# An expert loop's gated units ahead of a weight tile's halves, in two queues

## The chip, the cores and the metric

One core of a Trainium2 chip runs the kernel. Its engines, each with an instruction queue of its own, are TensorE (PE), VectorE (DVE), ScalarE (ACT), GpSimd (POOL) and SyncE (SP, which here only issues transfers). The metric is the device time of one execution in microseconds (us). A difference is told as the median of the runs of one kernel against that of the other.

## What is computed

The reference is a network in float32 on 256 tokens of width 1024: two blocks of convolution, state-space scan and a mixture of experts, and then four blocks of other mixers with dense feed-forward layers. The change lies in the mixture of experts, once in each of the first two blocks ("layer 0" and "layer 1" below):

```python
def expert(acc, ew):
    wg, wu, wd, cw = ew
    hid = jax.nn.silu(t @ wg) * (t @ wu)
    return acc + (cw[:, None] * (hid @ wd)).astype(acc.dtype), None
# 16 experts of width 256; each token is routed to two experts of one group of four
```

## The kernel before

**Split products.** A float32 matrix product is made of three products of a shorter float format. Each operand is cut into a high half (a rounded copy) and a low half (the operand less its high half): `mm3` (L752) issues high x high, high x low and low x high (L754, L755, L756). So each weight tile that arrives from memory is first split. ScalarE writes the high half (`make_high`, L1420, its copy is L1428), and then the low half is a subtraction (`make_low`, L416, its operation is L424). In the expert stages that subtraction is cut in two: VectorE takes the first 1024 columns, GpSimd the other 1024, both released by ScalarE's semaphore `high`. The tiles of the down projection are split in the same way by `make_down_high` (L1434) and `make_down_low` (L433), 512 columns on each of the two engines.

**Tokens by expert.** Tokens are scattered into 16 blocks of 128 rows, one block per expert. An expert's 256 hidden units are two slices of 128, so a layer has 32 slices: the even slice `j` and the odd slice `j + 1` of one expert are called a pair here. A slice has one gate-up weight tile (1 MB, 128 partitions x 2048) and one down tile (512 KB, 128 x 1024). The loop `slices_loop` (L435) runs `one(j, g)` on every engine; four slices are one turn of a hardware loop. Each engine runs its own list in its own order, and only semaphores tie them.

**TensorE's list** (`one`, L1096): at an even slice the rows of the next expert are transposed (`turn_rows`, L1062). Then the first half of the gate-up product of slice `j + 1` (12 matmuls), the transposition of the hidden rows of slice `j` (`turn_hidden`, L1079), the second half of the gate-up product of `j + 1`, and the down product of slice `j` (6 matmuls of 512 columns). The gate-up product of a slice waits for both low halves of its tile, VectorE's and GpSimd's (`low_ready`, L408).

**ScalarE's list** (`one`, L1653): the activation of the gate (L1655, releases `gate_act`), the high half of the tile of slice `j + 2` (L1428), the high half of the transposed hidden rows (L1659, waits for `hid_turned`, which TensorE's L1079 releases), at an even slice the high half of the next expert's rows (L1637), the high half of the next down tile (L1434), and at an odd slice `store`: it waits for the pair's down product, copies it out of PSUM (L1646) and issues a transfer (L1651).

**VectorE's list** (`one`, L2393): gate times up (L2395, releases `hid_raw`), the low half of the tile of slice `j + 2` (L424), the low half of the hidden rows (L2399, waits for `hid_high`, which L1659 releases; it releases `hidden`, for which the down product waits), the low half of the next expert's rows (L2390), the low half of the next down tile (L433).

**GpSimd's list** (`one`, L612): the transfer of an expert's rows (L610), its part of the low half of the tile of slice `j + 2` (L424), its part of the low half of the down tile of `j + 1` (L433).

Two buffers hold high halves (`HIGH`), four hold loaded tiles (`RING`). In the profile some names are those of the memory underneath: `border` is the activation `gact` and the raw hidden rows, `border_halves` the split hidden rows `hid`, `HT_halves` the split expert rows, `ssdb` the output rows, `zs_b` the arriving rows, `bank` a PSUM bank. The second expert stage of a layer, for overflowing experts, is skipped in this run: L1655 runs 64 times, 32 per layer.

Of the kernel before, what the change touches and what calls it, by code (L numbers as in the profile page):

```python
# [32 lines left out]
P = 128  # L33
# [29 lines left out]
RING = 4  # L63
QUAD = 32
HIGH = 2
TCOLS = 2 * P
# [134 lines left out]
def program(nc, dram, out, known):  # L201
# [4 lines left out]
    def sem(name):  # L206
        if name not in sems:
            sems[name] = ctx.enter_context(nc.semaphore(name))
            count[name] = 0
        return sems[name]  # L210
# [12 lines left out]
    def loop_base(name, key, total):  # L223

        sem(name)
        seen[name, key] = count[name]
        count[name] += total
        return seen[name, key]

    def base(name, key):  # L230
        sem(name)
        return known.get((name, key), 0)

    with ctx:
# [43 lines left out]
        ps = [ctx.enter_context(nc.psum_tensor(f"bank{b}", [P, 512], F32)) for b in range(8)]  # L278
# [15 lines left out]
        def view(buf, off, *shape):  # L294
            x = buf[:, off:off + int(np.prod(shape))]
            names = "abcd"[:len(shape)]
            if len(shape) == 1:
                return x
            return x.rearrange(f"p ({' '.join(names)}) -> p {' '.join(names)}",
                               **dict(zip(names[:-1], shape[:-1])))  # L300
# [30 lines left out]
        hid = view(border_r, 0, 2, 2, T)  # L331
# [8 lines left out]
        r = lambda x: x.bitcast(F32R)  # L340
# [75 lines left out]
        def make_low(eng, engine, c, g=0):  # L416

            at_ = slice(0, CUT[c]) if engine == "dve" else slice(CUT[c], TILE)
            if at_.start == at_.stop:
                return  # L420
            w, h = ring[SPLIT[c] % RING][:, at_], high[c % HIGH][:, at_]
            eng.wait_ge(sem("high"), c + 1 + RING * g)
            low = r(ring_r[SPLIT[c] % RING][:, at_])
            eng.tensor_tensor(low, w, h, ALU.subtract).then_inc(sem(f"low_{engine}"), 1)  # L424
# [985 lines left out]
        def _(act):  # L1410
# [9 lines left out]
            def make_high(c, g=0):  # L1420

                if c >= len(SPLIT):
                    return
                t = SPLIT[c]
                act.wait_ge(sem(f"tile_loaded{t % RING}"), 16 * (t // RING + 1) + 16 * g)
                if c >= HIGH:
                    act.wait_ge(sem("tile_free"), SPLIT[c - HIGH] + 1 + RING * g)
                nc.scalar.copy(r(high[c % HIGH][:]), ring[t % RING][:]).then_inc(sem("high"), 1)  # L1428

            def make_down_high(d, g=0):  # L1430
                act.wait_ge(sem(f"down_loaded{d % RING}"), 16 * (d // RING + 1) + 16 * g)
                if d >= HIGH or not isinstance(g, int):
                    act.wait_ge(sem("down_free"), d - HIGH + 1 + RING * g)
                nc.scalar.copy(r(dhigh[d % HIGH][:]), dring[d % RING][:]).then_inc(sem("down_high"), 1)  # L1434
# [190 lines left out]
            def experts(name, blocks, row0):  # L1625
                t0, c0, d0, slices = TILE_AT[name], SPLIT_AT[name], DOWN_AT[name], PER_BLOCK * blocks
                turned0, hid_turned0 = base("x_turned", name), base("hid_turned", name)
                taken0 = loop_base("out_taken", name, blocks)
                stored0 = [loop_base(f"y_stored{p}", name, 16 * blocks // 2) for p in range(2)]
                loop_base("gate_act", name, slices)  # L1630
                loop_base("x_high", name, blocks)
                loop_base("hid_high", name, slices)

                def split_rows(b, g):
                    act.wait_ge(sem("x_turned"), turned0 + b + 1 + RING // 2 * g)
                    for n in range(2):
                        i = nc.scalar.copy(r(xT[:, b % 2, 0, 4 * n:4 * n + 4, :].rearrange("p a b -> p (a b)")), ps[6 + n][:])  # L1637
                    i.then_inc(sem("x_high"), 1)

                def store(b, g):  # L1640

                    act.wait_ge(sem("down_free"), d0 + 2 * b + 2 + RING * g)
                    if stored0[b % 2] or b >= 2 or not isinstance(g, int):
                        act.wait_ge(sem(f"y_stored{b % 2}"), stored0[b % 2] + 16 * (b // 2) + 16 * g)
                    for n in range(2):
                        i = nc.scalar.copy(yrows[:, b % 2, n * D // 2:(n + 1) * D // 2], ps[2 * (b % 2) + n][:])  # L1646
                    i.then_inc(sem("out_taken"), 1)
                    act.wait_ge(sem("out_taken"), taken0 + b + 1 + RING // 2 * g)
                    dst = y_slots[row0 + P * b:row0 + P * b + P] if isinstance(g, int) else \
                        y_slots[bass.ds(row0 + P * b + 2 * P * g, P)]  # L1650
                    act.dma_start(dst, yrows[:, b % 2, :]).then_inc(sem(f"y_stored{b % 2}"), 16)  # L1651

                def one(j, g):  # L1653
                    act.wait_ge(sem("tile_free"), t0 + j + 1 + RING * g)
                    act_fn(gact[:, j % 2, 0:P], ps[4 + j % 2][:, 0:P], ACT.Silu).then_inc(sem("gate_act"), 1)  # L1655
                    if j + 2 < slices:
                        make_high(c0 + j + 2, g)
                    act.wait_ge(sem("hid_turned"), hid_turned0 + j + 1 + RING * g)
                    nc.scalar.copy(r(hid[:, j % 2, 0, 0:P]), ps[4 + j % 2][:, TCOLS:TCOLS + P]).then_inc(sem("hid_high"), 1)  # L1659
                    if j % 2 == 0 and j // 2 + 1 < blocks:  # L1660
                        split_rows(j // 2 + 1, g)
                    if j + 1 < slices:
                        make_down_high(d0 + j + 1, g)
                    if j % 2:
                        store(j // 2, g)

                if name[0] == "over":
                    for a in range(2):
                        make_high(c0 + a)
                make_down_high(d0)  # L1670
                split_rows(0, 0)
                slices_loop(act, slices, one, 0 if taken0 else 1)

            def moe(l, blocks):
# [246 lines left out]
        def _(dve):  # L1921
# [458 lines left out]
            def experts(name, blocks):  # L2380
                c0, d0, slices = SPLIT_AT[name], DOWN_AT[name], PER_BLOCK * blocks
                act0, high0, hid_high0 = (base(x, name) for x in ("gate_act", "x_high", "hid_high"))
                for n, total in (("x_split", blocks), ("hid_raw", slices), ("hidden", slices)):
                    loop_base(n, name, total)

                def split_rows(b, g):
                    dve.wait_ge(sem("x_high"), high0 + b + 1 + RING // 2 * g)
                    for n in range(2):
                        hi, lo = (xT[:, b % 2, i, 4 * n:4 * n + 4, :].rearrange("p a b -> p (a b)") for i in range(2))
                        i = tt(r(lo), ps[6 + n][:], hi, ALU.subtract)  # L2390
                    i.then_inc(sem("x_split"), 1)

                def one(j, g):  # L2393
                    dve.wait_ge(sem("gate_act"), act0 + j + 1 + RING * g)
                    tt(hrows[:, j % 2, :], gact[:, j % 2, 0:P], ps[4 + j % 2][:, P:TCOLS], ALU.mult).then_inc(sem("hid_raw"), 1)  # L2395
                    if j + 2 < slices:
                        make_low(dve, "dve", c0 + j + 2, g)
                    dve.wait_ge(sem("hid_high"), hid_high0 + j + 1 + RING * g)
                    tt(r(hid[:, j % 2, 1, 0:P]), ps[4 + j % 2][:, TCOLS:TCOLS + P], hid[:, j % 2, 0, 0:P], ALU.subtract)\  # L2399
                        .then_inc(sem("hidden"), 1)  # L2400
                    if j % 2 == 0 and j // 2 + 1 < blocks:
                        split_rows(j // 2 + 1, g)
                    if j + 1 < slices:
                        make_down_low(dve, "dve", d0 + j + 1, g)

                if name[0] == "over":
                    for a in range(2):
                        make_low(dve, "dve", c0 + a)
                make_down_low(dve, "dve", d0)
                split_rows(0, 0)  # L2410
                slices_loop(dve, slices, one)

            def moe(l, blocks):
# [533 lines left out]
```

## Time and profile before

| | |
|---|---|
| median of 3 runs | 2509.26 us (2508.42 to 2522.15) |
| the profiled execution | 2514.59 us, its span 2512.9 us |
| TensorE, VectorE, ScalarE, GpSimd busy | 2159.1, 1591.7, 1115.9, 475.6 us |
| loop of layer 0: GpSimd's first and last L424 start | 460.08 and 635.52 us |
| loop of layer 1: the same | 968.29 and 1153.02 us |

Busy time is the sum over instructions of one engine. A row of the trace's timeline has the start, the duration, the engine, the line, what it writes and reads, and in brackets how long the engine had been idle before it and what released it. Start times count from the start of the span.

### The profile page before, as it was taken

The numbers are of one execution on the slowest core, as the hardware profiler recorded it, in microseconds if no ns is written. First come the engines' busy times: TensorE is split into PE (matmuls) and PEld (weight loads), VectorE is DVE, ScalarE is ACT, GpSimd is POOL, SyncE is SP. The second block draws the span as 40 slices with busy tenths as digits, with TensorE's granted clock in tenths as the row PEclk, the third lists the DMA queues.
The fourth block names the chain that finished last, engine by engine and source line by source line (L and its number), as shares of the span: only waits on it lengthen the run. The fifth ranks groups of instructions, "written<-read, shape, count | busy, mean of one in ns | idle before, by whom it ended". The sixth has DMA issues, their size and how long they took to land.

```text
span 2512.9 us, 40162 instructions
## 1 busy us (share of the span) xinstructions
PE 2159.1 (86%) x15258; PEld 1899.4 (76%) x15268; DVE 1591.7 (63%) x2540; ACT 1115.9 (44%) x1628; POOL 475.6 (19%) x328
## 2 busy tenths in 40 slices
PE   5999886788489776876899999889997999899997
PEld 2776465677377475765878999779996899888997
DVE  2878655577468555764566776666667666556665
ACT  3224533566333634674444455224332433455332
POOL 1000002688300016884042021100000000000000
PEclk7999898899789888998899999999998999999999
DMA  6457812799445136995325467455543445333452
GB/s 253 168 202 270 283 67 92 275 344 342 169 150 197 39 118 238 329 324 212 134 101 210 169 211 240 163 187 186 191 175 134 143 175 209 123 113 118 177 192 82
DMA packets 103173, 471.48 MB, mean 188 GB/s; under 512 B 11520, under 2 KB 30208, under 8 KB 66048
## 3 DMA queue, kind: packets, MB, share of 16 engines
q1 hardware_dynamic: 84480, 404.79, 45.4%
q0 software_dynamic: 13232, 44.84, 4.7%
q10 hardware_dynamic: 5328, 20.07, 2.0%
q8 instruction: 86, 1.41, 0.2%
q14 instruction: 47, 0.39, 0.0%
HBM read 412.76 MB, written 54.79 MB: 186 GB/s over the span
## 4 chain that ended last, share of the span: by engine, by line
PE 42%; DVE 6%; ACT 2%; issue 1%; DVEq 1%; SPq 1%; DMA 0%; POOL 0%; ACTq 0%; POOLq 0%
PE bank L754 12%; PE bank L756 12%; PE bank L755 12%; DVE ring_halves L424 2%; ACT high L1428 1%; PE bank L1149 1%; PE bank L1283 1%; PE bank L1335 1%; PE bank L805 1%; PE bank L1316 1%; PE bank L1273 1%; PE bank L1260 1%; DVE dring_halves L433 0%; PE bank L1265 0%; PE bank L1264 0%
## 5 line engine op out<-in xcount | busy, mean ns | idle before, releaser
L754 PE MATMUL bank<-ssdb_halves,high 128*128 128x256 f32 (+1 forms) x2080 | 619.5, 298 | 51.1 <-DVE HT_halves L1967 18.6
L755 PE MATMUL bank<-HT_halves,high 128*128 128x256 f32 (+1 forms) x2096 | 619.6, 296 | 0.0
L756 PE MATMUL bank<-ssdb_halves,ring_halves 128*128 128x256 f32 (+1 forms) x2080 | 616.6, 296 | 0.0
L424 DVE TENSOR_TENSOR ring_halves<-ring,high 128x2048 fp32r<-128x2048 f32 (+1 forms) x230 | 482.3, 2098 | 195.6 <-ACT high L1428 194.4
L1428 ACT CAST high<-ring 128x2048 fp32r<-128x2048 f32 x230 | 437.5, 1903 | 217.6 <-PE bank L756 121.2
L754 PEld LDWEIGHTS bank<-ssdb_halves,high 128*128 128x128 f32 x2080 | 396.2, 190 | 70.7 <-issue 37.1
L755 PEld LDWEIGHTS bank<-HT_halves,high 128*128 128x128 f32 x2096 | 402.1, 192 | 8.9
L756 PEld LDWEIGHTS bank<-ssdb_halves,ring_halves 128*128 128x128 f32 x2080 | 396.5, 191 | 10.3
L424 POOL TENSOR_TENSOR ring_halves<-ring,high 128x1024 fp32r<-128x1024 f32 x66 | 224.7, 3404 | 651.7 <-ACT high L1428 651.7
L433 DVE TENSOR_TENSOR dring_halves<-dring,dhigh 128x1024 fp32r<-128x1024 f32 (+1 forms) x152 | 226.3, 1489 | 159.6 <-ACT dhigh L1434 159.1
L1434 ACT CAST dhigh<-dring 128x1024 fp32r<-128x1024 f32 x152 | 160.6, 1057 | 243.9 <-PE bank L756 243.9
L754 PE MATMUL bank<-border_halves,dhigh 128*128 128x256 f32 x704 | 201.9, 287 | 6.7 <-DVE border_halves L2444 6.7
L756 PE MATMUL bank<-border_halves,dring_halves 128*128 128x256 f32 x704 | 201.8, 287 | 0.0
L755 PE MATMUL bank<-border_halves,dhigh 128*128 128x256 f32 x704 | 201.4, 286 | 0.0
L756 PE MATMUL bank<-high,HT_halves 128*128 128x256 f32 x640 | 183.4, 287 | 0.0
L754 PE MATMUL bank<-high,HT_halves 128*128 128x256 f32 x512 | 156.7, 306 | 17.9 <-POOL ring_halves L424 10.9
L755 PE MATMUL bank<-ring_halves,HT_halves 128*128 128x256 f32 x512 | 145.6, 284 | 0.0
L754 PEld LDWEIGHTS bank<-border_halves,dhigh 128*128 128x128 f32 x704 | 135.2, 192 | 7.6 <-issue 7.2
L754 PE MATMUL bank<-HT_halves,high 128*128 128x256 f32 (+1 forms) x384 | 119.1, 310 | 20.9 <-DVE MIX_halves L2683 10.7
L756 PEld LDWEIGHTS bank<-border_halves,dring_halves 128*128 128x128 f32 x704 | 135.1, 192 | 0.0
L755 PEld LDWEIGHTS bank<-border_halves,dhigh 128*128 128x128 f32 x704 | 134.5, 191 | 0.0
L756 PEld LDWEIGHTS bank<-high,HT_halves 128*128 128x128 f32 x640 | 124.0, 194 | 0.0
(453 smaller groups left out, 3888.1 us busy)
## 6 DMA issues: line engine op xcount, KB each, us to landing
ring<-in_ffn SPq DMA_DIRECT2D x88, 1024.0 KB, 5.6
ring<-in_moe SPq DMA_DIRECT2D x64, 1024.0 KB, 7.4
ring<-in_ada SPq DMA_DIRECT2D x48, 1024.0 KB, 6.1
dring<-in_ffn_down SPq DMA_DIRECT2D x88, 512.0 KB, 3.7
dring<-in_moe_down SPq DMA_DIRECT2D x64, 512.0 KB, 4.7
ring<-in_foxin SPq DMA_DIRECT2D x24, 1024.0 KB, 4.9
ring<-in_win SPq DMA_DIRECT2D x22, 1024.0 KB, 7.7
zs_b<-x_slots POOLq DMA_DIRECT2D x32, 512.0 KB, 8.9
```

What stands on the lines that cost most here:

```text
L424: eng.tensor_tensor(low, w, h, ALU.subtract).then_inc(sem(f"low_{engine}"), 1)
L433: eng.tensor_tensor(low, w, h, ALU.subtract).then_inc(sem(f"down_low_{engine}"), 1)
L754: mm(o, a[0], b[0], start=first, stop=last and bool(kw), **kw)
L755: mm(o, a[0], b[1], start=False, stop=last and bool(kw), **kw)
L756: return mm(o, a[1], b[0], start=False, stop=last, **kw)
L805: i = mm(ps[7][:, 0:tok.stop - tok.start], k("mean1024"), sq[:, c, tok], start=c == 0, stop=c == KC - 1)
L1149: mm(o, b_one[:, i, (BATCH * c + q) % S5_HALF, :], e_blk[:, i, q, 0:STEP, :], start=q == 0 and i == 0, stop=False, skip_group_check=True)
L1260: mm(L[:, 0:384], r(splr[:, n, 0, h:h + 1]).to_broadcast([P, P]), r(fw[:, 0:384]), start=n == 0, stop=True, skip_group_check=True)
L1273: i = nc.tensor.transpose(ps[2 + h % 2][:, to * P:to * P + P], prob[:, h % 3, blk * P:blk * P + P], ident)
L1283: mm(o[q:q + HD, 0:T], vtok[:, 0, h * HD:h * HD + HD], probT[:, h % 2, 0:T], start=True, stop=False)
L1428: nc.scalar.copy(r(high[c % HIGH][:]), ring[t % RING][:]).then_inc(sem("high"), 1)
L1434: nc.scalar.copy(r(dhigh[d % HIGH][:]), dring[d % RING][:]).then_inc(sem("down_high"), 1)
```

## The change

In ScalarE's list of an expert slice the high half of the hidden rows (with its wait for `hid_turned`) is put ahead of the high half of the tile of slice `j + 2`. In VectorE's list the low half of the hidden rows (with its wait for `hid_high`) is put ahead of the low half of the tile of slice `j + 2`. TensorE's, GpSimd's and SyncE's lists are as before, and no instruction is added, removed or changed in size.

```diff
@@ ScalarE, experts @@
                     act.wait_ge(sem("tile_free"), t0 + j + 1 + RING * g)
                     act_fn(gact[:, j % 2, 0:P], ps[4 + j % 2][:, 0:P], ACT.Silu).then_inc(sem("gate_act"), 1)
+                    act.wait_ge(sem("hid_turned"), hid_turned0 + j + 1 + RING * g)
+                    nc.scalar.copy(r(hid[:, j % 2, 0, 0:P]), ps[4 + j % 2][:, TCOLS:TCOLS + P]).then_inc(sem("hid_high"), 1)
                     if j + 2 < slices:
                         make_high(c0 + j + 2, g)
-                    act.wait_ge(sem("hid_turned"), hid_turned0 + j + 1 + RING * g)
-                    nc.scalar.copy(r(hid[:, j % 2, 0, 0:P]), ps[4 + j % 2][:, TCOLS:TCOLS + P]).then_inc(sem("hid_high"), 1)
@@ VectorE, experts @@
                     tt(hrows[:, j % 2, :], gact[:, j % 2, 0:P], ps[4 + j % 2][:, P:TCOLS], ALU.mult).then_inc(sem("hid_raw"), 1)
-                    if j + 2 < slices:
-                        make_low(dve, "dve", c0 + j + 2, g)
                     dve.wait_ge(sem("hid_high"), hid_high0 + j + 1 + RING * g)
                     tt(r(hid[:, j % 2, 1, 0:P]), ps[4 + j % 2][:, TCOLS:TCOLS + P], hid[:, j % 2, 0, 0:P], ALU.subtract)\
                         .then_inc(sem("hidden"), 1)
+                    if j + 2 < slices:
+                        make_low(dve, "dve", c0 + j + 2, g)
```

## Rows read from the trace of the kernel before

**Rows 1.** The page: span and instructions.

```profile
span 2512.9 us, 40162 instructions
```

**Rows 2.** Busy time by stretch, both loops: PE, PEld, DVE, ACT, POOL; clock, DMA share, GB/s.

```profile
470.00:630.00 160.00, 135.78 (x924) 118.83 (x924) 118.94 (x131) 110.98 (x158) 138.93 (x66) 1.00 0.95 344
980.00:1140.00 160.00, 126.93 (x858) 110.58 (x857) 113.74 (x127) 113.22 (x157) 132.20 (x62) 1.00 0.92 325
```

**Rows 3.** Waits in layer 0, 470 to 630 us: total us, times, longest.

```profile
POOL ring_halves L424 <- ACT high L1428: 19.5, 13, 1.7
...
PE bank L754 <- DVE border_halves L2399: 16.4, 13, 1.3
...
PE bank L754 <- POOL ring_halves L424: 4.8, 12, 0.4
```

**Rows 4.** Timeline of ScalarE over one pair, even slice, odd slice, next pair.

```profile
530.94 1.89 ACT L1428 CAST high<-ring 128x2048 fp32r<-128x2048 f32 x1
532.73 0.27 ACT L1659 CAST border_halves<-bank 128x128 fp32r<-128x128 f32 x1
...
534.96 1.93 ACT L1428 CAST high<-ring 128x2048 fp32r<-128x2048 f32 x1
538.33 0.27 ACT L1659 CAST border_halves<-bank 128x128 fp32r<-128x128 f32 x1 [1.44 <-PE bank L1079]
538.49 1.05 ACT L1434 CAST dhigh<-dring 128x1024 fp32r<-128x1024 f32 x1
541.15 1.08 ACT L1646 COPY ssdb<-bank 128x512 f32<-128x512 f32 x2 [1.61 <-PE bank L756]
...
542.86 0.28 ACT L1655 ACTIVATE border<-bank 128x128 f32<-128x128 f32 x1 [0.64 <-ACT ssdb L1646]
```

**Rows 5.** Timeline of GpSimd over the same pair.

```profile
532.91 3.44 POOL L424 TENSOR_TENSOR ring_halves<-ring,high 128x1024 fp32r<-128x1024 f32 x1 [1.67 <-ACT high L1428]
...
538.00 3.39 POOL L424 TENSOR_TENSOR ring_halves<-ring,high 128x1024 fp32r<-128x1024 f32 x1
```

**Rows 6.** Timeline of VectorE over the same pair.

```profile
532.86 1.23 DVE L424 TENSOR_TENSOR ring_halves<-ring,high 128x1024 fp32r<-128x1024 f32 x1 [1.50 <-ACT high L1428]
...
539.57 2.37 DVE L433 TENSOR_TENSOR dring_halves<-dring,dhigh 128x512 fp32r<-128x512 f32 x1 [0.25 <-ACT dhigh L1434]
```

**Rows 7.** Timeline of TensorE over the same pair, and its next transposition.

```profile
531.42 0.33 PE L1079 MATMUL bank<-con,border 128*128 128x128 f32 x1 [0.34 <-DVE border L2395]
...
534.44 0.47 PE L754 MATMUL bank<-dhigh,border_halves 128*128 128x512 f32 x1 [1.26 <-DVE border_halves L2399]
...
536.48 0.38 PE L754 MATMUL bank<-high,HT_halves 128*128 128x256 f32 x1 [0.40 <-POOL ring_halves L424]
...
538.01 0.27 PE L1079 MATMUL bank<-con,border 128*128 128x128 f32 x1
...
543.51 0.14 PEld L1079 LDWEIGHTS bank<-con,border 128*128 128x128 f32 x1 [0.32 <-DVE border L2395]
```

**Rows 8.** GpSimd's first and last L424 of 30, layer 0, then layer 1.

```profile
460.08 3.44 POOL L424 TENSOR_TENSOR ring_halves<-ring,high 128x1024 fp32r<-128x1024 f32 x1 [8.23 <-ACT high L1428]
...
635.52 3.36 POOL L424 TENSOR_TENSOR ring_halves<-ring,high 128x1024 fp32r<-128x1024 f32 x1
...
968.29 3.45 POOL L424 TENSOR_TENSOR ring_halves<-ring,high 128x1024 fp32r<-128x1024 f32 x1 [8.55 <-ACT high L1428]
...
1153.02 3.38 POOL L424 TENSOR_TENSOR ring_halves<-ring,high 128x1024 fp32r<-128x1024 f32 x1
```

**Rows 9.** ScalarE's timeline: the first L1659 of layer 0.

```profile
460.33 0.27 ACT L1659 CAST border_halves<-bank 128x128 fp32r<-128x128 f32 x1 [0.33 <-PE bank L1079]
```

**Rows 10.** ScalarE's timeline in layer 1: one of 6 table loads in its loop.

```profile
1016.69 1.28 ACT L1655 ACT_TABLE_LOAD   x1 [0.97 <-ACT ssdb L1646]
```

**Rows 11.** TensorE's timeline, layer 1's first gate-up product: every third weight load.

```profile
961.62 0.33 PEld L754 LDWEIGHTS bank<-high,HT_halves 128*128 128x128 f32 x1
...
962.26 0.33 PEld L754 LDWEIGHTS bank<-high,HT_halves 128*128 128x128 f32 x1
```

## The prediction

> **What bounds the kernel now.** The page gives the span, 2512.9 us [rows 1], and shows TensorE busiest over the whole, but the change touches only the two expert loops, so the next view is busy time by stretch [rows 2]. There TensorE is busy 135.8 of 160 us in layer 0 and 126.9 in layer 1, GpSimd 138.9 and 132.2, at a granted clock of 1.00. No engine is full: work is handed round. The waits say by whom [rows 3]: in 13 pairs TensorE waits 16.4 us for the low half of the hidden rows (1.26 us a pair, at the even slice's down product) and 4.8 us for GpSimd's L424; GpSimd waits 19.5 us for ScalarE's high half (1.50 a pair).
>
> The timelines of one pair show which of these closes a circle. GpSimd's L424 of the even slice runs 532.91 to 536.35 [rows 5], and TensorE's next gate-up product starts at 536.48, 0.13 us later [rows 7]. From that start the circle goes on: the odd slice's down product ends and ScalarE's copy-out starts at 541.15, the next activation at 542.86 [rows 4], a high half follows, and GpSimd's next L424. So TensorE's 1.26 us before the even down product (534.44) is not on the circle: had that product started earlier, TensorE would still have waited for GpSimd's 536.35. What counts is when GpSimd gets a high half. The odd slice's high half is made at 534.96 [rows 4], long before GpSimd takes it at 538.00 [rows 5]. It is work done ahead, and it takes GpSimd's second L424 off the circle. The length of the loop is read on GpSimd: 30 L424 per layer, from the first start to the last 635.52 - 460.08 = 175.44 us in layer 0 and 1153.02 - 968.29 = 184.73 in layer 1 [rows 8], so 12.10 and 12.74 us per pair (29 steps are 14.5 pairs).
>
> **The change, part by part.** Nothing is added or removed: all 40162 instructions stay [rows 1], and so do the transfers.
>
> *ScalarE.* Before, the high half of slice j + 2's tile followed the activation. Now it stands behind L1659 of slice j, which waits for TensorE's transposition L1079, and TensorE issues that only after the first half of the gate-up product of slice j + 1. That product needs the low halves of tile j + 1. So the tile's halves of one slice now wait for those of the slice before:
>
> GpSimd's L424 for j + 1, gate-up product of j + 1 (first half), transposition j, high hidden half j, high tile half j + 2, GpSimd's L424 for j + 2.
>
> Each link has a duration:
> - L424 start on GpSimd to gate-up start on TensorE: 536.48 - 532.91 = 3.57 [rows 5, 7].
> - gate-up start to transposition start, with no wait between: 538.01 - 536.48 = 1.53 [rows 7].
> - transposition to L1659: 538.33 - 538.01 = 0.32 [rows 4, 7].
> - L1659 to the next instruction on ScalarE: 538.49 - 538.33 = 0.16 [rows 4].
> - high tile half to L424 on GpSimd: 532.91 - 530.94 = 1.97 [rows 4, 5].
>
> The sum is 7.55 us per slice, 15.10 per pair, and this circle holds at even and odd slices alike. Against 12.10 that is +3.00 a pair; about 1.0 of it would be there if only the even high half were late, the rest is the odd half's lead, which is lost: ScalarE will reach L1659 of the odd slice early and stand there about 3 us before it may make the tile's half.
>
> Does the rest fit inside 15.10? Count from the odd gate-up start as 0. ScalarE's high tile half starts at 1.53 + 0.32 + 0.16 = 2.01, the down tile's 1.80 later (532.73 - 530.94, [rows 4]) and ends at 4.86. The down product ends at about 541.15 - 536.48 = 4.67 [rows 4, 7]. So the copy-out starts near 4.9, the next activation 1.71 later (542.86 - 541.15) at 6.6, and the transposition could start 0.65 after that (543.51 - 542.86, [rows 4, 7]), at 7.25. It is due at 7.55 + 1.53 = 9.08. The slack is 1.8 us.
>
> *VectorE.* Its L424 waited for the high tile half anyway, 1.50 us at even slices [rows 6], so L2399 ahead of it costs nothing by itself. What VectorE must keep is the gate-times-up L2395 ahead of each transposition. Its low down half L433 seems to run only when GpSimd's L424 is over: it started at 539.57, ended at 541.94 [rows 6], 0.55 after GpSimd's L424 (538.00 + 3.39 = 541.39, [rows 5]). In the new order that gives 7.42 + 0.55 = 8.0 for its end, and 8.3 for the transposition, due 9.08: 0.8 us of slack. If that cover went, each missing tenth would lengthen a slice by a tenth.
>
> *TensorE* gains the 1.26 us before the even down product [rows 3], and stands longer before the next gate-up product: a gain off the circle, priced at zero. *SyncE* issues the next tile when the gate-up product is done, so later; the stretch moves 344 GB/s at a DMA share of 0.95 now [rows 2] and would move about 344 x 12.1 / 15.1 = 276. *GpSimd's* own row transfers follow its L433 and are later by as much as the pair.
>
> *Layer 1* has a table load before every fourth activation, 1.28 us and 0.97 instead of 0.64 ahead of it [rows 4, 10]: 1.61 us that now lie on the circle (this is the 9.3 us by which its loop is longer). In the new order they fall into the 1.8 us of slack, so this loop too takes 7.55 a slice.
>
> *Edges.* The first L424 of a layer waits for the first L1659: 460.33 + 0.16 + 1.97 = 462.46 against 460.08, +2.38 [rows 8, 9]. Behind the last L424 there are no more tile halves, and the order is indifferent; the transposition no longer waits for the activation behind the copy-out, about -0.3.
>
> *Sum.* 29 x 7.55 = 218.95 a layer. Layer 0: +43.5 + 2.4 - 0.3 = +45.6. Layer 1: +34.2 + 2.4 - 0.3 = +36.3. Together +82 us, on the span of 2512.9 a span of 2595. The profiled run's 2514.59 is 5 above the median 2509.26, so the median forecast is 2591. The links repeat to within about 0.1 us, over 58 steps that is 6 either way, and the slack at VectorE may be short by 0.2 in some slices: its own range is 2578 to 2605.
>
> **One rule against the trace.** VectorE's L424 for even slices takes 1.23 us beside GpSimd's, while its smaller L433 takes 2.37 when it starts inside one [rows 6]. The Trainium skill, "GPSIMD Engine Reference", section "8. Key points", says that GpSimd shares its SBUF interfaces with VectorE and contends with VectorE instructions that have two SBUF inputs. Both L424 are of that kind; the trace agrees for L433. Read strictly, by that rule a VectorE L424 that comes second to the port would wait out GpSimd's; the time is that of the port rival below, 2659, against 2591 by the order in the rows.
>
> **The rivals.**
> - *The clock falls.* TensorE would idle some 3 us before each odd gate-up product and 2 before each even one. Before the change it idles up to 1.3 in the pair shown and kept 1.00 in both loops [rows 2, 7]. At half clock, 1.2 GHz, three weight loads take 0.64 us (962.26 - 961.62, [rows 11]), so the twelve of the first half product 2.56 against the 1.53 above, which has the start-up in it: about 1.1 longer. In every second slice: 29 x 1.1 = +32, 2623; in all: +64, 2655. Chance 0.10.
> - *The port.* GpSimd's L424 starts 0.05 us behind VectorE's [rows 5, 6]. If it came first, VectorE's would end after 3.39 + 1.23 = 4.6 us where GpSimd's now ends after 3.44: 1.2 us more in each of 58 slices, +68, 2659. Both engines wait for the same release in the new order as in the even slices now, so: 0.04.
> - *Only the even half is late.* Were the odd high half still ahead of need, the even one would start at 531.42 + 0.32 + 0.16 = 531.90 instead of 530.94 [rows 4, 7]: 0.96 x 32 = +31, 2540. The trace has the odd transposition at 538.01, behind a product that needs GpSimd, so: 0.05.
> - *Faster.* The low hidden half comes earlier and TensorE's 1.26 us a pair go: 32 x 1.26 = -40, 2469. It is what happens if the following gate-up product doesn't wait for GpSimd. In 12 of 13 pairs it did [rows 3], and 0.13 us behind it. Chance 0.03.
> - *No difference* (another queue's wait than read here sets the pair): 0.03.
>
> **How the numbers follow.** The forecast has the remaining 0.75. The range takes in its own, the half-way clock case and a little of a smaller loss: 2570 to 2628, leaving out the full clock case, the port and the cases below, some 0.17. About 1% is what can be told from no change. Slower by over 1% (above 2534): 0.75 + 0.10 + 0.04 + 0.05 = 0.94; same 0.03; faster 0.03.
>
> **What would show it.** In the changed kernel's trace: GpSimd's L424 starts at an even 7.55 us, each 1.97 behind a high half on ScalarE; ScalarE waits about 3 us for the odd L1079 and under 2 for the even one; the wait of TensorE for L2399 is gone, and its wait before each gate-up product ends with GpSimd's L424, up to 3 us long; layer 0 and layer 1 take the same time, with table loads that delay nobody; the clock stays 1.00. Wrong it would be if GpSimd's L424 of odd slices still started right behind its L433, if VectorE's L2395 were what TensorE waits for, or if weight loads came at 0.64 us for three.

## The result, and the profile after

The changed kernel takes 2605.78 us (median of 4 runs, 2602.34 to 2615.14) against 2509.43: a ratio of 1.0378, 95% interval 1.0335 to 1.0421, some 95 us slower. The forecast was 2591, with a range of 2570 to 2628.

The page of the changed kernel: the span is 89.6 us longer with the same number of instructions [rows 1].

```profile
span 2602.5 us, 40162 instructions
```

Busy time by stretch in the two loops, the columns as in [rows 2]:

```profile
470.00:630.00 160.00, 119.94 (x713) 108.24 (x713) 90.17 (x101) 87.00 (x123) 106.71 (x50) 0.87 0.74 265
1035.00:1195.00 160.00, 118.17 (x729) 106.13 (x728) 90.89 (x104) 93.42 (x128) 108.62 (x53) 0.90 0.77 269
```

Every engine is less busy: TensorE issues 713 matmuls in 160 us instead of 924. In layer 0 the transfers fell from 344 to 265 GB/s. And the granted clock is no longer 1.00 but 0.87 and 0.90. (The second stretch starts later than in [rows 2], as the loop of layer 1 does.)

The waits in layer 0, 470 to 690 us, show who stands still:

```profile
ACT border_halves L1657 <- PE bank L1079: 85.3, 28, 4.7
POOL ring_halves L424 <- ACT high L1428: 72.8, 28, 3.8
...
PE bank L754 <- POOL ring_halves L424: 49.9, 25, 2.9
```

ScalarE's copy of the hidden rows (now L1657) waits for the transposition 3.0 us a slice, GpSimd waits 2.6 us a slice for its high half (before, 1.5 once a pair, [rows 3]), and TensorE's gate-up product waits for GpSimd in nearly every slice, up to 2.9 us. The wait for the low hidden half (16.4 us in [rows 3]) is gone from the list. The chain is the one that was forecast. One link after the other, from the timelines of GpSimd, TensorE and ScalarE:

```profile
566.87 3.39 POOL L424 TENSOR_TENSOR ring_halves<-ring,high 128x1024 fp32r<-128x1024 f32 x1 [3.63 <-ACT high L1428]
...
570.31 0.19 PEld L754 LDWEIGHTS bank<-high,HT_halves 128*128 128x128 f32 x1 [1.85 <-POOL ring_halves L424]
...
571.84 0.27 PE L1079 MATMUL bank<-con,border 128*128 128x128 f32 x1
...
572.15 0.27 ACT L1657 CAST border_halves<-bank 128x128 fp32r<-128x128 f32 x1 [2.30 <-PE bank L1079]
572.31 1.91 ACT L1428 CAST high<-ring 128x2048 fp32r<-128x2048 f32 x1
...
574.31 3.39 POOL L424 TENSOR_TENSOR ring_halves<-ring,high 128x1024 fp32r<-128x1024 f32 x1 [1.86 <-ACT high L1428]
```

From one L424 to the next this is 574.31 - 566.87 = 7.44 us. The link from L424 to the gate-up product is 570.31 - 566.87 = 3.44, 0.13 shorter than the forecast took from [rows 5, 7]; the others are within 0.03 of it. But the step after it is longer. GpSimd's next L424 starts at 582.27, 7.96 later. TensorE's product in between ran at half clock for a while:

```profile
577.82 0.19 PEld L754 LDWEIGHTS bank<-high,HT_halves 128*128 128x128 f32 x1 [3.31 <-issue]
...
579.68 0.33 PEld L754 LDWEIGHTS bank<-high,HT_halves 128*128 128x128 f32 x1
580.32 0.33 PEld L754 LDWEIGHTS bank<-high,HT_halves 128*128 128x128 f32 x1
```

Behind an idle time of 3.31 us the weight loads of L754 come, after the first few, every 0.64 us, the pace of [rows 11], instead of every 0.35. The steps between GpSimd's L424 in layer 0, worked out from the starts, in us:

```
7.72 7.47 8.80 7.75 7.50 7.42 7.51 7.43 7.92 7.48 8.83 7.46 8.70 7.44 7.96
7.45 8.82 7.46 8.73 7.43 8.00 7.46 8.83 7.44 8.85 7.56 7.53 8.77 7.61
```

Sixteen lie between 7.42 and 7.61; the others go up to 8.85. The two loops take 229.3 and 224.2 us from first to last L424, against 175.4 and 184.7 [rows 8] and a forecast of 218.95 each.

### The profile page after: what moved, and what is told of

It reads as the page before. It is cut to its first block, busy times and chain, and to the rows that moved or that the text cites. A ratio compares the mean times of both kernels' runs of the same rounds, so it can differ in the third digit from the quotient of the medians.

```text
span 2602.5 us, 40162 instructions
## 1 busy us (share of the span) xinstructions
PE 2196.9 (84%) x15258; PEld 1938.5 (74%) x15268; DVE 1588.8 (61%) x2540; ACT 1117.7 (43%) x1628; POOL 475.7 (18%) x328
## 4 chain that ended last, share of the span: by engine, by line
PE 41%; DVE 5%; ACT 2%; issue 1%; DVEq 1%; SPq 0%; DMA 0%; POOL 0%; ACTq 0%; POOLq 0%
PE bank L754 12%; PE bank L756 12%; PE bank L755 12%; DVE ring_halves L424 2%; ACT high L1428 1%; PE bank L1149 1%; PE bank L1283 1%; PE bank L1335 1%; PE bank L1316 1%; PE bank L1273 1%; PE bank L805 0%; PE bank L1260 0%; DVE dring_halves L433 0%; PE bank L1265 0%; PE bank L1264 0%
## 5 line engine op out<-in xcount | busy, mean ns | idle before, releaser
L754 PE MATMUL bank<-ssdb_halves,high 128*128 128x256 f32 (+1 forms) x2080 | 619.1, 298 | 49.2 <-DVE HT_halves L1967 18.4
L424 DVE TENSOR_TENSOR ring_halves<-ring,high 128x2048 fp32r<-128x2048 f32 (+1 forms) x230 | 456.5, 1986 | 238.9 <-ACT high L1428 237.7
L754 PEld LDWEIGHTS bank<-ssdb_halves,high 128*128 128x128 f32 x2080 | 395.9, 190 | 68.8 <-issue 37.6
L424 POOL TENSOR_TENSOR ring_halves<-ring,high 128x1024 fp32r<-128x1024 f32 x66 | 223.9, 3392 | 748.7 <-ACT high L1428 748.7
L433 DVE TENSOR_TENSOR dring_halves<-dring,dhigh 128x1024 fp32r<-128x1024 f32 (+1 forms) x152 | 245.3, 1614 | 153.5 <-ACT dhigh L1434 153.2
L754 PE MATMUL bank<-high,HT_halves 128*128 128x256 f32 x512 | 177.1, 346 | 128.7 <-POOL ring_halves L424 115.6
L1434 ACT CAST dhigh<-dring 128x1024 fp32r<-128x1024 f32 x152 | 160.1, 1054 | 244.3 <-PE bank L756 244.3
L754 PEld LDWEIGHTS bank<-high,HT_halves 128*128 128x128 f32 x512 | 116.1, 227 | 149.7 <-issue 107.2
L754 PE MATMUL bank<-border_halves,dhigh 128*128 128x256 f32 x704 | 201.1, 286 | 6.7 <-DVE border_halves L2444 6.7
L756 PE MATMUL bank<-high,HT_halves 128*128 128x256 f32 x640 | 201.4, 315 | 0.0
L755 PE MATMUL bank<-ring_halves,HT_halves 128*128 128x256 f32 x512 | 163.7, 320 | 0.0
L756 PEld LDWEIGHTS bank<-high,HT_halves 128*128 128x128 f32 x640 | 142.9, 223 | 0.0
L754 PEld LDWEIGHTS bank<-border_halves,dhigh 128*128 128x128 f32 x704 | 134.4, 191 | 7.6 <-issue 7.2
L754 PE MATMUL bank<-HT_halves,high 128*128 128x256 f32 (+1 forms) x384 | 119.8, 312 | 20.5 <-DVE MIX_halves L2241 10.7
```

The lines of the kernel that those rows point to most:

```text
L433: eng.tensor_tensor(low, w, h, ALU.subtract).then_inc(sem(f"down_low_{engine}"), 1)
L754: mm(o, a[0], b[0], start=first, stop=last and bool(kw), **kw)
L755: mm(o, a[0], b[1], start=False, stop=last and bool(kw), **kw)
L756: return mm(o, a[1], b[0], start=False, stop=last, **kw)
```

## The experiments

All ratios are to the kernel before as run beside it on the same chip. In these runs it took 2515 to 2519 us, up to 9 more than the 2509 on which the expected times rest, so ratios are what to compare. "Loop" is the time from GpSimd's first L424 of a layer to its last, in the profiled execution; the clock is that of two stretches inside the loops, 480 to 620 and 1040 to 1140 us. Outside the loops single executions differ: between the two loops one execution of the changed kernel took 329.4 us, another 339.1. So the loops are compared by their own length.

| kernel | ratio (95%) | loops, us | clock in loops |
|---|---|---|---|
| before | 1 | 175.4, 184.7 | 1.00, 1.00 |
| changed | 1.0378 (1.0335 to 1.0421) | 229.3, 224.2 | 0.88, 0.90 |
| changed, again | 1.0396 (1.0374 to 1.0418) | 226.9, 224.4 | 0.90, 0.93 |
| ScalarE's part alone | 1.0528 (1.0509 to 1.0546) | 241.3, 247.2 | 0.91, 0.90 |
| VectorE's part alone | 1.0421 (1.0397 to 1.0446) | 241.5, 231.0 | 0.80, 0.91 |
| even slices only | 1.0303 (1.0279 to 1.0327) | 211.7, 216.8 | 0.87, 0.88 |
| odd slices only | 1.0070 (1.0052 to 1.0087) | 190.0, 195.3 | 0.91, 0.96 |
| changed, waits filled | 1.0337, then 1.0311 (1.0290 to 1.0332) | 216.7, 216.8, then 216.6, 216.8 | 1.00, 1.00 |
| even only, waits filled | 1.0152 (1.0099 to 1.0204) | 189.4, 198.5 | 1.00, 1.00 |
| high half a slice early | 0.9961 (0.9935 to 0.9987) | 169.5, 174.9 | 0.98, 1.00 |
| the same, VectorE's old order | 1.0039 (1.0020 to 1.0058) | 178.9, 188.0 | 1.00, 1.00 |
| changed, VectorE splits all | 1.0293 (1.0277 to 1.0308) | by VectorE's L424: 212.1, 221.6 | 0.87, 0.88 |
| early, VectorE splits all | 0.9967 (0.9950 to 0.9984) | by VectorE's L424: 169.5, 179.7 | 1.00, 0.97 |

**ScalarE's part alone.**

```diff
@@ ScalarE, experts: as in the change; VectorE as before @@
+                    act.wait_ge(sem("hid_turned"), hid_turned0 + j + 1 + RING * g)
+                    nc.scalar.copy(r(hid[:, j % 2, 0, 0:P]), ps[4 + j % 2][:, TCOLS:TCOLS + P]).then_inc(sem("hid_high"), 1)
                     if j + 2 < slices:
                         make_high(c0 + j + 2, g)
```

> Only ScalarE's list is changed; VectorE's is as before. Theory A (ScalarE's order carries the loss: each high tile half now waits for the transposition of its own slice): GpSimd's L424 again starts every 7.4 to 8.0 us in both loops, and the time is 2595 to 2615, within 0.5% of the changed kernel's 2606. VectorE's low hidden half now ends some 1.5 us after its L424 has begun, so the odd down product starts about 5.4 us after its gate-up product instead of 3.1, and the next expert's rows push the following gate-up product back by up to 0.5. Theory B (the two lists cost about half each): some 2557.

2651.66 us, 1.5% above the changed kernel and outside what either theory gave. Waits, 480 to 620 us:

```profile
PE bank L754 <- DVE border_halves L2399: 38.8, 17, 2.3
```

The wait for the low hidden half is back at every slice, 2.3 us each. The expectation priced this side effect at 0.5, too low: with L2399 behind VectorE's L424 the odd down product ends later, the next expert's rows are transposed after it, and the next gate-up product is no longer ready when GpSimd is: steps up to 9.36 us alternate with 7.53 in the middle of layer 0's loop. The long steps have half pace in them too:

```profile
561.83 1.91 PE L1062 MATMUL bank<-con,zs_b 128*128 128x128 f32 x8
```

These eight transpositions of rows take 1.04 us at 567.66 in the changed kernel. How the extra 35 us of the two loops divide between the later product and the clock was not measured. So ScalarE's part alone brings the whole loss and more, and VectorE's part, put on top of it, gives back about 1.5%.

**VectorE's part alone.**

```diff
@@ VectorE, experts: as in the change; ScalarE as before @@
                     dve.wait_ge(sem("hid_high"), hid_high0 + j + 1 + RING * g)
                     tt(r(hid[:, j % 2, 1, 0:P]), ps[4 + j % 2][:, TCOLS:TCOLS + P], hid[:, j % 2, 0, 0:P], ALU.subtract)\
                         .then_inc(sem("hidden"), 1)
+                    if j + 2 < slices:
+                        make_low(dve, "dve", c0 + j + 2, g)
```

> Only VectorE's list is changed; ScalarE makes the high tile half ahead of the hidden one as before. VectorE now comes to its L424 about 0.4 us after GpSimd has started its own. Theory P (a VectorE subtraction with both operands in SBUF waits until GpSimd's running one is over): VectorE's L424 takes 3 to 4 us and ends 1.1 after GpSimd's, which holds the gate-up product back by 1.1 at even slices and up to 0.8 at odd ones, so 32 x 1.1 to 32 x 1.9 = 35 to 61 us, 2545 to 2570. Theory N (the two engines run side by side): VectorE's L424 ends at 1.7 us after GpSimd's start, long before GpSimd's, and the time is 2500 to 2512.

1.0421, 109 us above the kernel before where theory P had 35 to 61. Timelines of GpSimd, VectorE and TensorE:

```profile
562.99 2.39 POOL L424 TENSOR_TENSOR ring_halves<-ring,high 128x1024 fp32r<-128x1024 f32 x1 [5.64 <-ACT high L1428]
...
563.32 3.14 DVE L424 TENSOR_TENSOR ring_halves<-ring,high 128x1024 fp32r<-128x1024 f32 x1
...
566.38 1.27 DVE L2390 TENSOR_TENSOR HT_halves<-bank,HT_halves 128x512 fp32r<-128x512 f32 x2
...
567.71 0.19 PEld L754 LDWEIGHTS bank<-high,HT_halves 128*128 128x128 f32 x1 [2.97 <-DVE HT_halves L2390]
```

VectorE comes 0.33 us after GpSimd, and its L424 takes 3.14 us: it ends 1.08 after GpSimd's 565.38. GpSimd's takes 2.39, not 3.4. So the two subtractions take turns, the first to come runs alone, and the other's duration contains its wait. The Trainium skill, "GPSIMD Engine Reference", section "8. Key points", states that the two engines share SBUF interfaces and contend where VectorE has two SBUF inputs; the trace agrees, 3.14 against 1.23 [rows 6]. Theory N falls, theory P holds with its price too low. One thing that it left out stands in the same rows: the next expert's low half (L2390) is queued behind, and the gate-up product waits for it too, 1.3 us more. Two others stand beside them. The clock is 0.80 in layer 0, the lowest of all runs. And gate times up (L2395) comes late, behind an L433 that takes 2.89 us, so that the transposition waits for it; from 480 to 620 us:

```profile
PEld bank L1079 <- DVE border L2395: 13.7, 16, 1.5
```

The shares of the three were not told apart.

**Even slices only, odd slices only.**

```diff
@@ ScalarE, even-only; VectorE likewise; odd-only with 1 and 0 exchanged @@
-                    if j + 2 < slices:
+                    if j + 2 < slices and j % 2 == 1:
                         make_high(c0 + j + 2, g)
                     act.wait_ge(sem("hid_turned"), hid_turned0 + j + 1 + RING * g)
                     nc.scalar.copy(r(hid[:, j % 2, 0, 0:P]), ps[4 + j % 2][:, TCOLS:TCOLS + P]).then_inc(sem("hid_high"), 1)
+                    if j + 2 < slices and j % 2 == 0:
+                        make_high(c0 + j + 2, g)
```

> The new order in both lists at even slices only, the old one at odd slices. Theory A: the odd high tile half keeps its lead, so a pair pays only the 0.96 us by which the even half is late: 32 x 0.96 = +31, 2535 to 2546, and GpSimd's L424 of odd slices starts right behind its L433. Theory B (every slice moved costs the same): half of 96, 2557. The granted clock stays at 1.00 in the loops.

> The new order in both lists at odd slices only. Theory A: the odd high half waits for the odd transposition, but the even one is made right behind the activation again and GpSimd works on without a wait: its L424, its L433 and a transfer, 5.6 us from one L424 to the next, then 7.55 over TensorE and ScalarE back to the odd one, 13.15 a pair against 12.10 and 12.74. So +15 in layer 0, +6 to +13 in layer 1, 2530 to 2540. Together with the even-only kernel that is some 60 us, against 96 for both: the loss is not a sum of two. Theory B: half of 96, 2557.

Odd only came out as expected, at 2537.03 us: loops +14.6 and +10.6 us, steps 5.6 and 6.9 to 7.7 in layer 0. Even only did not: 2592.29 us. The order is as foreseen (odd L424 5.05 us after the even one, right behind L433), but the pairs of layer 0 take 13.3 to 15.8 us where the expected 0.96 on top of 12.10 gives 13.06, and the clock is 0.87, not 1.00. A long pair, weight loads of TensorE:

```profile
583.72 0.29 PEld L754 LDWEIGHTS bank<-high,HT_halves 128*128 128x128 f32 x1 [3.30 <-issue]
584.32 0.33 PEld L754 LDWEIGHTS bank<-high,HT_halves 128*128 128x128 f32 x1
...
589.01 0.33 PEld L754 LDWEIGHTS bank<-dhigh,border_halves 128*128 128x128 f32 x1
```

Again an idle time of 3.30, then 0.64 us per three. In this kernel's circle the whole odd gate-up product counts, 583.72 to 589.01 = 5.29 us instead of 3.1.

**The waits filled.** To tell the clock from any other cause, TensorE gets work on zeros that nobody reads.

```diff
@@ TensorE, experts, one(j, g) @@
                     down(j, g)
+                    for _ in range(16 if j % 2 else 30):
+                        mm(ps[4 + j % 2][:, TCOLS + P:], zeros[:, 0:P], zeros[:, 0:P], start=True, stop=True)
```

(In the even-only kernel: 0 and 30.)

> The changed kernel with 30 small matmuls on zeros (128 columns, two-byte operands, into PSUM columns that nothing reads) behind TensorE's even down products and 16 behind the odd ones, so that part of its wait for GpSimd's L424 is filled. Nothing else differs, and they end before the wait does. Theory C (some 20 us of the loss is the lower clock in the product that follows a wait): the granted clock in the loops rises from 0.87 to 0.91 towards 1.00, GpSimd's L424 keeps an even 7.4 to 7.5 us, and the time is 2582 to 2592. Rival (the steps of 8.0 to 8.8 us come from something else, such as port contention): the steps stay, 2600 to 2610.

> The even-only order (2592 us, pairs of 13.3 to 15.8) with 30 of the small matmuls behind each even down product. Its circle holds the whole odd gate-up and down product, so half clock costs it 2.2 us and more in a pair. Theory C: with the clock kept, pairs take 13.1 to 13.3, and the time is 2540 to 2552. Rival (the 14.3 us pair is a wait that was overlooked): no change, 2585 to 2597.

Busy time by stretch of the changed kernel with its waits filled, from the second set of runs:

```profile
470.00:630.00 160.00, 136.08 (x1235) 122.32 (x1236) 95.74 (x107) 89.20 (x128) 114.76 (x55) 1.00 0.79 278
1035.00:1195.00 160.00, 136.94 (x1242) 122.91 (x1241) 95.11 (x107) 97.83 (x134) 113.62 (x54) 1.00 0.78 276
```

The clock is 1.00, all 29 steps of layer 0 lie between 7.43 and 7.52, and both loops take 216.7 us: extra work made them 12.6 and 7.4 us shorter. Yet the first median was 2599.69, outside the expected 2582 to 2592: in the profiled execution the loops are 20 us shorter and the stretches outside them 18 longer than in the changed kernel's. So it was run again beside the changed kernel:

> The changed kernel, unaltered, beside the next one on the same chip, since the stretches outside the two loops differed by 10 to 20 us between the single executions profiled so far, as much as the effect of the clock that is to be read. 1.035 to 1.040 of the kernel before. In its loops the steps of GpSimd's L424 spread from 7.4 to 8.8 us again.

> The changed kernel with the filling matmuls, unaltered from the run before. Theory C: its loops take 433 to 435 us together at a granted clock of 1.00 against some 450 to 455 of the changed kernel, and the median is 12 to 22 us below the changed kernel's of this same job, if the stretches outside are alike. Rival: the filling costs outside the loops what it gives inside, and the two medians lie within 8 us.

2618.57 against 2594.72: 24 us, with the loops 17.9 us apart; the other 6 lie outside them, and nothing here assigns them to the clock in the loops. The even-only kernel falls from 1.0303 to 1.0152, its pairs to 12.9 to 13.4 in layer 0, around the 13.06. So the clock costs the changed kernel 18 to 20 us and the even-only one some 40 (its loops go from 428.5 to 387.9), since there a whole product stands on the circle.

The clock also hides a result. By the ratios, odd only (0.7%) and even only (3.0%) seem to add up to the changed kernel's 3.8%. With the waits filled, the loops say otherwise: even only costs 27.7 us, both together 73, and odd only, measured with its clock below 1.00, at most 25.1. So at least 20 us come only when both halves are late.

**The opposite edit.** If the lead of the high half is what counts, more lead should gain.

```diff
@@ ScalarE, experts, one(j, g); make_high(c0 + 2) ahead of the loop @@
-                    if j + 2 < slices:
-                        make_high(c0 + j + 2, g)
...
                     if j + 1 < slices:
                         make_down_high(d0 + j + 1, g)
+                    if j + 3 < slices:
+                        make_high(c0 + j + 3, g)
                     if j % 2:
                         store(j // 2, g)
```

> The opposite of the change on ScalarE: the high tile half is made one slice earlier, for slice j + 3 at the end of slice j, ahead of the copy-out; VectorE's list is that of the changed kernel (low hidden half first). ScalarE's copy-out, its activation and the table loads leave the circle. GpSimd then is bound by its own work, 5.1 + 5.1 + 0.6 = 10.8 us a pair, the transfers by 344 x 12.1 / 10.8 = 385 GB/s, near the most that this kernel reaches in any stretch. 11.0 to 11.6 us a pair, so -16 in layer 0 and -25 in layer 1: 2455 to 2485. Against it: VectorE's L424 now often starts inside one of GpSimd's, as in the run of VectorE's part alone; if that costs more than 1 us a pair the time is back at 2500 to 2520.

> As the run before it, but VectorE's list is that of the kernel before (low tile half first). VectorE's L424 waits for GpSimd's running subtraction with the low hidden half queued behind it, so the down product waits up to 3 us for it. 2470 to 2520, slower than with the hidden half first.

0.9961 and 1.0039. The first is faster than the kernel before, by 0.4%, less than half of the least that was expected; its loops are 5.9 and 9.8 us shorter, where 16 and 25 were expected. Its waits, 480 to 620 us:

```profile
POOL dring_halves L433 <- ACT dhigh L1434: 27.1, 14, 2.7
...
PEld bank L1079 <- DVE border L2396: 15.1, 12, 2.6
...
ACT high L1428 <- DMA ring<-in_moe: 9.2, 6, 2.4
```

ScalarE now waits for the tiles themselves: the stretch moves 356 GB/s at a DMA share of 0.98. GpSimd's largest wait is for the down tile's high half, which comes late where L1434 stands behind L1657, and TensorE's is for gate times up (now L2396). The circle seems to have moved to the transfers and to the hidden rows; no run here parts the two. With VectorE's old order the gain is gone altogether (2522.82 us, just above the expected range): TensorE waits again for the low hidden half, 19.0 us in 12 pairs.

**VectorE splits all.** `LOW_BOTH = ()` gives VectorE both parts of every low half.

> The changed kernel, but VectorE makes the whole low half of each expert tile and down tile (and of the router's tile); GpSimd makes none. Theory P: of the 3.39 us of GpSimd's L424 only 2.39 is its own work, as the run of VectorE's part alone showed, the rest is waiting for VectorE's 1.1 at the shared port; a whole tile takes VectorE 2.1 to 2.2. The link from high half to gate-up product goes from 5.4 to about 4.2, so odd slices take about 6.2 us instead of 7.43; at even ones the next expert's rows (1.28) come in behind and take it back. Pairs of 13.6 instead of 14.9, more where the clock holds: 40 to 60 us below the changed kernel, 2545 to 2570. Rival (the two engines do share the work): VectorE's doubled part makes it slower, over 2610.

> ScalarE's high tile half one slice early, VectorE in the order of the kernel before and making all low halves, GpSimd none. Nothing waits at the port any more. VectorE has 4.4 us of work a slice, TensorE 4.9, ScalarE 5.0, the transfers 5.5 to 5.6 at 385 GB/s, so pairs of 11.0 to 11.4 against 12.10 and 12.74: 2455 to 2480, faster than the kernel before by 1.2 to 2.2%. Rival: VectorE's queue, with the low hidden half behind a 2.1 us subtraction, holds the down product as before, 2490 to 2515.

On the changed kernel, 2589.28 against 2618.57 beside it: faster by 29 us with one engine's help taken away. VectorE and TensorE in one pair:

```profile
569.51 2.29 DVE L424 TENSOR_TENSOR ring_halves<-ring,high 128x2048 fp32r<-128x2048 f32 x1 [1.52 <-ACT high L1428]
571.73 1.28 DVE L2390 TENSOR_TENSOR HT_halves<-bank,HT_halves 128x512 fp32r<-128x512 f32 x2
...
573.06 0.19 PEld L754 LDWEIGHTS bank<-high,HT_halves 128*128 128x128 f32 x1 [3.29 <-DVE HT_halves L2390]
```

2048 columns take VectorE 2.29 us alone; shared out, the last of them came 3.39 us after the start. That the rows' low half then takes 1.28 back at even slices is seen too. The gain is 29 instead of 40 to 60. The clock stayed at 0.87, which is the likely reason: undisturbed pairs of layer 0 take 6.29 + 7.48 = 13.77 us, near the 13.6 expected, but its loop takes 212.1, and 14.5 such pairs would take 200. This kernel was not run with its waits filled. The early kernel with VectorE alone takes 2509.28 us, 0.9967: no better than with the shared halves (0.9961), at a DMA share of 0.98 in layer 0. Both beat the kernel before by 0.3 to 0.4%, neither by the 1 to 2% expected. What shares the circle there beside the transfers was not settled.

## Why the prediction was right

- **The circle** (L424, half a product, transposition, hidden half, high half, L424): right, link by link. Forecast 7.55 us a slice, measured 7.43 to 7.53 with the waits filled; the loops then take 216.7 us against 218.95. The order alone costs 216.6 + 216.8 - 360.2 = +73 us in the loops, forecast +78. ScalarE's waits for L1079 in undisturbed slices are 3.3 and 2.3 to 2.5 us, forecast some 3 and under 2.
- **The odd half's lead**: right, by the runs of each half alone. The even halves by themselves cost 27.7 us in the loops with the clock kept, 0.96 a pair, just the price that the prediction gave to a late even half. The rest of the 73, more than the odd halves cost by themselves (25.1), comes when the odd half's lead goes as well. Neither half alone costs half of the 73, so that every slice moved costs the same is refuted.
- **The first L424**: +2.4 us forecast. From the first activation it is 464.88 - 460.31 = 4.57 instead of 460.08 - 457.93 = 2.15, +2.42.
- **The table loads of layer 1** fell into slack: with the waits filled the loops of both layers are equal to 0.2 us, where [rows 8] had them 9.3 apart.
- **VectorE's slack**: it held. Among the waits from 470 to 690 us TensorE's for L2395 does not appear. VectorE's own part of the change is needed all the same: with L2399 left in its old place (ScalarE's part alone) TensorE waits 2.3 us a slice for it, and the kernel is another 1.5% slower.
- **The clock**: the term that was mis-sized. The prediction took 1.00 and put the lower clock among the rivals with 0.10 and +32 for every second slice. It happened in 24 of 58 steps, mostly in part of a product, and cost 20 us. Two of the prediction's own signs say so: the clock did not stay at 1.00, and weight loads came at 0.64 us for three, which it had named as a sign of being wrong. The forecast argued from idle times up to 1.3 us in [rows 7]; the new ones are up to 3.3 us. The trace of before, outside the loops, shows that such a wait can go either way. Busy time by stretch there, the columns as in [rows 2]; in the first pair TensorE's weight loads stand idle for 3.02 us, in the second for 3.20:

```profile
57.70:60.70 3.00, 0.45 (x2) 0.01 (x1) 3.00 (x4) 0.53 (x2) 0.00 (x0) 1.00 0.00 0
61.50:63.50 2.00, 1.94 (x5) 0.86 (x4) 2.00 (x6) 1.33 (x4) 0.00 (x0) 0.50 0.00 0
1598.60:1601.80 3.20, 0.25 (x3) 0.05 (x1) 3.20 (x4) 2.84 (x2) 0.00 (x0) 1.00 0.57 184
1601.80:1604.00 2.20, 2.12 (x18) 2.15 (x19) 2.20 (x3) 0.34 (x1) 0.00 (x0) 1.00 0.51 216
```

  The first falls from 1.00 to 0.50, the second keeps 1.00. So on these rows the case deserved more than 0.10, at a price between 0 and 32.
- **The port**: no part in the changed kernel's loss (VectorE's L424 still comes first, 1.23 us), but it is inside the circle. About 1.0 of the 3.57 us from L424 to the gate-up product is GpSimd's wait for VectorE, which the prediction priced as GpSimd's own work.

The two errors have opposite signs: 78 - 73 = 5 too much for the order, 20 too little for the clock. Together they make the 15 us by which 2591 fell short of 2605.78. The range held by what it took in for a clock that falls in part: without a clock case it ended at 2605.

## What to carry over

Before a small, urgent step is put ahead of a long one in a queue, ask whether the long one was early on purpose. Here the hidden half gained nothing, since the next product waited for a tile's halves anyway, and the tile's half lost a lead of a whole slice. Then follow the freed or late step around the loop until it meets itself; that sum, taken from one pair of the trace, gave the loops' length at full clock within about 1%. And where a new order lets TensorE stand for some microseconds, its next product may run slower, as it did here, so price that product at both clocks.

## What the runs showed of the hardware

- In the loops of before TensorE's weight loads stood idle up to 1.97 us (in layer 1) at a clock of 1.00. In the changed kernel, after idle times of 3.3 us, they went at half pace (0.64 us for three instead of 0.35) in many cases but not in all, and from different points of the product on. The length of one wait doesn't settle it: this product ran at half pace behind 2.18 us, while the one behind 3.32 us at 515.05 kept full pace.

```profile
681.28 0.28 PEld L754 LDWEIGHTS bank<-high,HT_halves 128*128 128x128 f32 x1 [2.18 <-issue]
...
681.86 0.33 PEld L754 LDWEIGHTS bank<-high,HT_halves 128*128 128x128 f32 x1
```

  With 46 small matmuls on zeros per pair the granted clock in the loops was 1.00.
- Of two subtractions with both operands in SBUF, one on VectorE and one on GpSimd, the later one stretches by the rest of the earlier one: GpSimd's 128x1024 takes 2.39 us alone and 3.39 behind VectorE's, VectorE's takes 1.23 and 3.14. Splitting a 128x2048 tile between them took 3.39 us, VectorE alone 2.29.
